# Gate/up RMS norm with squares summed by three token thirds and the factor spread from 96 partitions

## The reference

```
def rmsnorm(x, g):
    y = xf * lax.rsqrt(jnp.mean(xf * xf, axis=-1, keepdims=True) + EPS)
    return (y * g).astype(x.dtype)
def ffn_half(x, g, wg, wu, wd):
    h = rmsnorm(x, g)
    return x + 0.5 * ((jax.nn.silu(h @ wg) * (h @ wu)) @ wd)
```

## Time and profile before

| | us |
|---|---|
| runs | 2058.07, 2057.37, 2061.0 (median 2058.07) |
| profiled execution: its time | 2061.27 |
| its span, first to last instruction | 2059.5 |
| TensorE busy | 2031.5 (99%) |
| VectorE busy | 1683.0 (82%) |
| ScalarE busy | 978.1 (47%) |
| GpSimd busy | 359.7 (17%) |

### The profile page before, as it was taken

The page is one execution under the profiler, slowest core; times in us unless marked ns, Lnnn a source line. Parts: engine busy times, 40 slices in busy tenths (PEclk is TensorE's granted clock), DMA queues, the critical chain, the costliest instruction groups (busy, mean ns, idle before and its releaser), DMA issues. The chain is left out here.

```text
span 2059.5 us, 41110 instructions
## 1 busy us (share of the span) xinstructions
PE 2031.5 (99%) x15435; PEld 1975.0 (96%) x15435; DVE 1683.0 (82%) x2481; ACT 978.1 (47%) x1776; POOL 359.7 (17%) x219
## 2 busy tenths in 40 slices
PE   8999999999999999999989999999999999999998
PEld 7999999999889999999989999999997899999998
DVE  5999998756666999998899999976657589999975
ACT  6544453324545544463465655533345474444532
POOL 0322200033011222200022222001321112222000
PEclk8999999999999999999999999999999999999999
DMA  4232332352112222322223222324321122232331
GB/s 133 83 102 84 99 92 79 92 129 65 45 54 83 83 88 96 97 88 86 78 83 102 88 95 79 112 79 118 95 68 32 55 82 91 94 102 79 94 96 65
DMA packets 236727, 178.35 MB, mean 87 GB/s; under 512 B 35808, under 2 KB 231616, under 8 KB 236608
## 3 DMA queue, kind: packets, MB, share of 16 engines
q1 hardware_dynamic: 231712, 170.36, 27.8%
q10 hardware_dynamic: 4896, 6.36, 1.1%
HBM read 170.12 MB, written 3.62 MB: 84 GB/s over the span
## 5 line engine op out<-in xcount | busy, mean ns | idle before, releaser
L1471 PE MATMUL pair<-t_parts,chunk_high 128*128 128x288 f32 x4592 | 916.7, 295 | 6.3 <-POOL chunk_low L827 2.6
L1471 PEld LDWEIGHTS pair<-t_parts,chunk_high 128*128 128x128 f32 x4592 | 736.8, 188 | 8.0 <-POOL chunk_low L827 3.2
L1471 PE MATMUL pair<-t_parts,chunk_low 128*128 128x288 f32 x2296 | 677.7, 295 | 0.0
L1471 PEld LDWEIGHTS pair<-t_parts,chunk_low 128*128 128x128 f32 x2296 | 431.4, 188 | 0.0
L827 POOL TENSOR_TENSOR chunk_low<-set_raw,chunk_high 128x512 fp32r<-128x512 f32 x164 | 236.6, 1453 | 872.1 <-ACT chunk_high L926 872.1
L926 ACT ACTIVATE chunk_high<-chunk_sum 128x512 fp32r<-128x512 f32 x328 | 203.8, 630 | 372.5 <-DVE chunk_sum L2024 190.4
L821 POOL TENSOR_TENSOR w_low<-raw,w_high 128x1024 fp32r<-128x1024 f32 (+2 forms) x48 | 115.7, 2414 | 620.7 <-ACT w_high L874 620.7
L2036 DVE TENSOR_TENSOR chunk_low<-chunk_sum,chunk_high 128x512 fp32r<-128x512 f32 x328 | 214.5, 695 | 9.2 <-ACT chunk_high L926 1.9
L1418 PE MATMUL pair<-hidden_high,w_high 128*128 128x288 f32 x896 | 191.9, 296 | 0.0
L1418 PE MATMUL pair<-hidden_high,w_low 128*128 128x288 f32 x896 | 191.9, 296 | 0.0
L1418 PE MATMUL pair<-hidden_low,w_high 128*128 128x288 f32 x896 | 191.8, 296 | 0.0
(11 more groups left out here) (304 smaller groups left out, 3727.0 us busy)
## 6 DMA issues: line engine op xcount, KB each, us to landing
set_raw<-in_w_up_dram SPq DMA_DIRECT2D x44, 1024.0 KB, 5.3
set_raw<-in_w_gate_dram SPq DMA_DIRECT2D x44, 1024.0 KB, 5.3
raw<-in_w_down_dram SPq DMA_DIRECT2D x64, 448.0 KB, 3.8
down_raw<-in_w_down_dram SPq DMA_DIRECT2D x16, 1024.0 KB, 5.4
raw<-in_w_in_dram SPq DMA_DIRECT2D x20, 512.0 KB, 3.9
raw<-in_w_in_dram SPq DMA_DIRECT2D x16, 256.0 KB, 3.9
raw<-in_w_out_dram SPq DMA_DIRECT2D x8, 512.0 KB, 3.5
raw<-in_w_out_dram SPq DMA_DIRECT2D x16, 256.0 KB, 4.1
```

The lines of the kernel that those rows point to most:

```text
L1471: mm = nc.tensor.matmul(out, c[:, j, p, :], tr[p // 2][:, seat(p), x, t, :], start=p == 0 and n == 0, stop=p == KP - 1 and n == 2)
```

## The change

The tokens are cut into three thirds of 192 (`THIRD_T`). The sum of squares of third g goes to partitions 32g to 32g+31, 24 matmuls of 192 columns in place of 16 of 288. ScalarE takes the root of these 96 x 192 sums straight from PSUM into `sq_tmp`, in the place of the copy L1201. VectorE takes the reciprocal of 96 x 192 in place. Three matmuls spread it: the weights are one column of the identity (row 32g), read 128 times, the moving operand is `sq_tmp[0:96]`. The copy of partial sums, the matmuls L1537, the diagonals and the five matmuls with them go away. The positions of the reciprocal in VectorE's order and of the `keep_scale` copies in ScalarE's stay; the copies are cut at 384 tokens, not at 512, and need no factor. In the block phase `mean_square` is three matmuls on `sq_sum`, and the spread is two matmuls in the first part and one in the second.

```
-            def root(count, sums, parts):
+            def root(count, sums):
                 act.wait_ge(sum_done, 2 * count + 2)
-                nc.scalar.activation(root_tok[:, 0:4], sums[:, 0:4], ACT.Sqrt, bias=eps[:, 0:1], scale=float(parts)).then_inc(root_done, 1)
-                nc.scalar.activation(root_tok[0:DEC, 4:5], sums[0:DEC, 4:5], ACT.Sqrt, bias=eps[0:DEC, 0:1], scale=float(parts)).then_inc(root_done, 1)
-            def spread(count):
-                act.wait_ge(rms_ready, count + 1)
-                for t, (t0, n) in enumerate(TILES):
-                    ins = nc.scalar.activation(sq_tmp[0:n, t0:t0 + n], ident[0:n, 0:n], ACT.Copy, scale=root_tok[0:n, t:t + 1])
-                ins.then_inc(spread_made, 1)
+                nc.scalar.activation(sq_tmp[0:96, 0:THIRD_T], sums, ACT.Sqrt, bias=eps[0:96, 0:1]).then_inc(root_done, 2)
...
 (plain_tiles, ScalarE)
                 combined_of(0)
-                act.wait_ge(sum_done, 2 * ph + 1)
-                nc.scalar.activation(two(rms[0:96, :]), halves(3)[0:96], ACT.Copy).then_inc(parts_kept, 1)
+                root(ph, ps[3][0:96, 0, 0:THIRD_T])
                 free(3)
                 plain_chunks(q + 1, 1, 1)
...
                 combined_of(2)
-                root(ph, ps[ALONE][:, 0, 0:5], D_MODEL // 32)
                 combined_of(3)
-                spread(3 * layer + 2 * w)
                 chunk(q + 2, 0, A11)
...
+                def sum_thirds(pair, half, parts):
+                    for m, src in enumerate(parts):
+                        for g in range(3):
+                            mm = nc.tensor.matmul(ps[pair][32 * g:32 * g + 32, half, 0:THIRD_T], mean_d[:, 0:32], src[:, g * THIRD_T:(g + 1) * THIRD_T],
+                                                  start=m == 0, stop=m == len(parts) - 1)
+                    mm.then_inc(sum_done, 2)
+                def spread_thirds(part, pair, half):
+                    pe.wait_ge(rms_ready, 3 * layer + 2 * w + 1)
+                    for g in ((0, 1), (2,))[part]:
+                        col = (g % 2) * THIRD_T
+                        mm = nc.tensor.matmul(ps[pair][:, half, col:col + THIRD_T], ident[0:96, 32 * g:32 * g + 1].broadcast_to([96, P]),
+                                              sq_tmp[0:96, 0:THIRD_T], start=True, stop=True)
+                    mm.then_inc(scale_made, 1)
...
 (gate_up, TensorE)
+                    sum_thirds(3, 0, squares)
                     plain_tile(1, 0)
-                    pe.wait_ge(parts_kept, plain_before(layer, w) + 1)
-                    for t, (t0, n) in enumerate(TILES):
-                        mm = nc.tensor.matmul(ps[ALONE][0:n, 0, t:t + 1], rms[0:96, t0:t0 + n], mean_d[0:96, 0:1], start=True, stop=True)
+                    pe.wait_ge(root_done, 2 * ph + 2)
                     plain_tile(1, 1)
                     pe.wait_ge(left_made, set_number(layer, w, 0, 0) + 2)
-                    for t, (t0, n) in enumerate(TILES):
-                        dst = ps[FIRST][:, 0, t0:t0 + n] if t < 4 else ps[FIRST][:, 1, 0:n]
-                        mm = nc.tensor.matmul(dst, mean_d[0:n, :], sq_tmp[0:n, t0:t0 + n], start=True, stop=True)
+                    for part in range(2):
+                        spread_thirds(part, FIRST, part)
...
 (make_scale, VectorE)
-                nc.vector.reciprocal(root_tok[:, :], root_tok[:, :]).then_inc(rms_ready, 1)
+                nc.vector.reciprocal(sq_tmp[0:96, 0:THIRD_T], sq_tmp[0:96, 0:THIRD_T]).then_inc(rms_ready, 1)
```

More of the change, by code:

```diff
@@ L33 @@
 HALF = NT // 2
+THIRD_T = NT // 3
 KD = D_MODEL // P
@@ L926, in chunk @@
                 nc.scalar.activation(ch[:, j], src, ACT.Copy).then_inc(chunk_high, 1)
-            def root(count, sums, parts):
+            def root(count, sums):
                 act.wait_ge(sum_done, 2 * count + 2)
-                nc.scalar.activation(root_tok[:, 0:4], sums[:, 0:4], ACT.Sqrt, bias=eps[:, 0:1], scale=float(parts)).then_inc(root_done, 1)
-                nc.scalar.activation(root_tok[0:DEC, 4:5], sums[0:DEC, 4:5], ACT.Sqrt, bias=eps[0:DEC, 0:1], scale=float(parts)).then_inc(root_done, 1)
-            def spread(count):
-                act.wait_ge(rms_ready, count + 1)
-                for t, (t0, n) in enumerate(TILES):
-                    ins = nc.scalar.activation(sq_tmp[0:n, t0:t0 + n], ident[0:n, 0:n], ACT.Copy, scale=root_tok[0:n, t:t + 1])
-                ins.then_inc(spread_made, 1)
+                nc.scalar.activation(sq_tmp[0:96, 0:THIRD_T], sums, ACT.Sqrt, bias=eps[0:96, 0:1]).then_inc(root_done, 2)
             def keep_scale(ph, part, pair, half):
                 act.wait_ge(scale_made, 2 * ph + part + 1)
-                dst, src = (rms[:, 0:SEQ], ps[pair][:, 0, :]) if part == 0 else (rms[:, SEQ:NT], ps[pair][:, half, 0:DEC])
-                nc.scalar.activation(dst, src, ACT.Copy, scale=float(D_MODEL)).then_inc(rms_spread, 1)
+                dst, src = (rms[:, 0:2 * THIRD_T], ps[pair][:, 0, 0:2 * THIRD_T]) if part == 0 else (rms[:, 2 * THIRD_T:NT], ps[pair][:, half, 0:THIRD_T])
+                nc.scalar.activation(dst, src, ACT.Copy).then_inc(rms_spread, 1)
             def gate_up(layer, w, base_slot):
@@ L992, in during @@
                     if opens and b == 0:
-                        root(ph, ps[ALONE][:, 1, 0:5], 1)
+                        root(ph, ps[ALONE][0:96, 1, 0:THIRD_T])
                     for j in (S1, S2, S3, S4):
                         chunk(q + 1, 1 - b, j)
-                        if opens and b == 1 and j == S1:
-                            spread(3 * layer + 2 * w)
                         if opens and b == 1 and j == S4:
@@ L1477, in one_set @@
                             spread_scale(int(j == A22))
+                def sum_thirds(pair, half, parts):
[4 more added lines that the diff above has]
+                    mm.then_inc(sum_done, 2)
                 def mean_square():
                     pe.wait_ge(sq_added, 2 * KD * layer + 1)
-                    for t, (t0, n) in enumerate(TILES):
-                        mm = nc.tensor.matmul(ps[ALONE][0:n, 1, t:t + 1], sq_sum[:, t0:t0 + n], mean_d[:, 0:1], start=True, stop=True)
-                    mm.then_inc(sum_done, 2)
-                def spread_scale(part):
[L1488 to L1492, removed]
+                    sum_thirds(ALONE, 1, [sq_sum])
+                def spread_thirds(part, pair, half):
[5 more added lines that the diff above has]
+                    mm.then_inc(scale_made, 1)
+                def spread_scale(part):
+                    if part:
                         pe.wait_ge(rms_spread, 2 * ph + 1)
-                        mm = nc.tensor.matmul(ps[ALONE][:, 0, 0:DEC], mean_d[0:DEC, :], sq_tmp[0:DEC, SEQ:NT], start=True, stop=True)
-                    mm.then_inc(scale_made, 1)
+                    spread_thirds(part, ALONE, 0)
                 def plain_tile(b, n):
@@ L1525, in gate_up @@
                     pe.wait_ge(h_ready, x_count + KD)
[L1526 to L1532, removed]
-                    plain_tile(1, 0)
-                    pe.wait_ge(parts_kept, plain_before(layer, w) + 1)
-                    pe.wait_ge(left_made, set_number(layer, w, 0, 0) + 1)
-                    for t, (t0, n) in enumerate(TILES):
-                        mm = nc.tensor.matmul(ps[ALONE][0:n, 0, t:t + 1], rms[0:96, t0:t0 + n], mean_d[0:96, 0:1], start=True, stop=True)
-                    mm.then_inc(sum_done, 1)
+                    sum_thirds(3, 0, squares)
+                    plain_tile(1, 0)
+                    pe.wait_ge(root_done, 2 * ph + 2)
                     plain_tile(1, 1)
-                    pe.wait_ge(root_done, 2 * ph + 2)
-                    pe.wait_ge(spread_made, ph + 1)
                     pe.wait_ge(left_made, set_number(layer, w, 0, 0) + 2)
-                    for t, (t0, n) in enumerate(TILES):
-                        dst = ps[FIRST][:, 0, t0:t0 + n] if t < 4 else ps[FIRST][:, 1, 0:n]
-                        mm = nc.tensor.matmul(dst, mean_d[0:n, :], sq_tmp[0:n, t0:t0 + n], start=True, stop=True)
-                    mm.then_inc(scale_made, 2)
+                    for part in range(2):
+                        spread_thirds(part, FIRST, part)
                     one_set(1, 0)
```

3 lines of the change are left out of this document (1 added, 2 removed).

## The result

The changed kernel took 2063.64 us (median of 9 runs, 2061.78 to 2066.48), the kernel before 2057.62 us (9 runs, 2056.74 to 2061.0) on the same chip. The ratio is 1.003, 95% interval 1.0021 to 1.0039: slower by 0.3%, where 2056.6 us and no change had been forecast. The two profiled executions hide it: their spans are 2060.0 after and 2059.5 before, because before's took 2061.27 us, longer than any of its 9 runs, and after's 2061.78, its fastest.

A forecast was written before the change was run, and what follows sets the result against it. TensorE, busy 2031.5 of 2059.5 us, was taken as the bound, VectorE setting the block phase's pace. Three plain phases gaining 0.75 us each, less 0.8 in the block phase, gave -1.45, say 1.5: 2056.6 us, range 2052.8 to 2060.4.

The forecast's parts named there:

- The sums: TensorE, plain phase: 48 records run as 16 trios of 0.16, 2.6 us against 2.9 to 3.0, 0.4 us earlier.
- rival B: Sums on TensorE: three groups don't overlap at 192 columns, 3.9 us, 0.9 more than before; 2060.5 us; chance 0.08.
- The table load: ScalarE ahead of the root: the 1.28 us load runs before the wait, in idle time, so it hides.
- Root and reciprocal: Plain phase: ScalarE's root of 192 columns takes 0.42 us, VectorE's reciprocal of 192 columns 1.35 us.
- GpSimd's collision: Plain phase: GpSimd's second low part holds up VectorE's T3 low part, about 1.2 us lost; A12 gains 0.75, not 1.9.
- Rival A: GpSimd and VectorE in plain phases: their collision doesn't cost, A12 starts at 54.15; -5 us, 2053.1 us; chance 0.22.
- rival C: VectorE, plain and block phases: the reciprocal excludes GpSimd, A12 0.7 us late three times; +4.1 us, 2062.2 us; chance 0.08.
- The wait before A12: TensorE, each plain phase: waits about 1.9 us for ScalarE's copy, where 0.74 on GpSimd stood.
- a cover: TensorE's 1.9 us wait before A12, taken also as room for a slower weight load in the spread.
- The block phase: Longer reciprocal where VectorE has no room: A11 of the next set 0.8 us later; first copy's wait about 3 us.

The follow-up runs named there:

- the load in its place: Changed kernel with the root's semaphore increment 1 instead of 2, so the table load stands ahead of the wait: 2057.12 us, ratio 0.9995 to the kernel before.
- the held low part: On top of the root's increment of 1, GpSimd's low part of A12 held until VectorE's combination S2 is made, in plain phases: 2057.67 us, ratio 0.9999.
- Filled: Changed kernel plus small float32 matmuls on TensorE, 5 before A12 in each plain phase, 6 before the block phase's second spread: 2060.84 us, ratio 1.001.

## Why the prediction was wrong

The forecast was 1.5 us of gain; the loss was 6.0. Its steps:

- **The sums**: 2.6 us for the block forecast, 2.7 measured; the trios overlap. Right, rival B falls.
- **The table load**: the step that failed. "So it hides" was read off a root that carried its wait itself, and off idle time ahead of the copy. That there was time to hide it was right; that the load would use this time was not checked against the new instruction's form. The forecast did name the price, "if it ran behind the wait, 1.28 us would be lost": it measured 1.34, three times, 4.0 us. With the load in its place A12 came 0.95 us earlier by the trace, where 0.75 was forecast.
- **Root and reciprocal**: 0.42 and 1.34 us, forecast 0.42 and 1.35. With the load in its place the spread (1.14 us) waits for nothing, as forecast; with the load behind the sums it waited 0.85.
- **GpSimd's collision**: that the two engines hold each other up was right, who waits and for how long was not. It was to stretch the low part of T3 by 1.2 us; T3, T4 and S1 ran at their own pace, GpSimd's low parts took 1.97 us longer, and S2 was stretched by 0.92. Both stand ahead of the copies, so the effect on A12 was nearly the same. Rival A, that it costs nothing, falls by the held low part; rival C, that the reciprocal excludes GpSimd, falls with the reciprocal at 1.34.
- **The wait before A12**: forecast at 1.9 us, measured 1.99. That they agree is in part luck: the wait began and ended later than forecast, and with the load in its place it was 1.72. And it was priced as idle time alone and even called a cover. It was the clock's price that was missing: no term, bound or rival spoke of what TensorE's granted clock does behind such a wait. Filled, with all else equal, the kernel is 2.8 us faster by the medians.
- **The block phase**: 0.9 us by the trace against 0.8, and the wait "about 3 us" was 2.74. Here too the fall of the clock, about 1.4 us, came on top.

The sum, redone with what was measured: three plain phases at +0.39 us, the block phase at +0.9, and three falls at 1.4 to 1.5 us (the one near 1040 us costs nothing) give +6.3 to +6.6 us. The traces give +6.4 over the four phases, and 6.0 was measured between the medians. The profiled spans differ by only 0.5 us because the rest of the program hides 5.9: the early rise of the clock (1.46), and 2.8 and 1.6 us where the trace before has its own falls, near 472 us (with a wait of 2.40 us that was 1.56 after) and near 1551 us.

The Trainium skill, "TensorE: Matmul & The Clock Gate", section "HAM oscillation — how this bites in real kernels", tells of a kernel in which TensorE's waits between pieces of work bring the lower clock, so that each piece starts cold. The waits of that kernel are longer than those here, so it doesn't promise a fall behind 2 us. The traces show such falls, with 0.50 behind the waits that end at 55.01 and 1066.14 us, though not each time. Had it been weighed beside the forecast's own wait of 1.9 us, a slower rival could have stood there.

## What to carry to other kernels

Price a new wait of TensorE twice: its own length, and the granted clock behind it; look for places where the kernel before already waits two microseconds and read the clock after them, in more than one execution, since it falls in some and not in others. When an activation changes tables and waits, look in the trace at which of the two instructions, load or activation, has the wait; a small activation of the same table ahead of it puts the load where it is free. And before a chain is made shorter, look at which instruction ends the wait at its far end: here the order of two short copies was worth 6.6 us on top of the new form, which by itself, with the load in its place, was not clearly faster than the old one (1.0 us, inside the scatter); in the old form the same order brought nothing clear.

## What the runs showed of the hardware

- An activation with a wait and an increment of 2, where it needs a new table, had its wait on the table load; with an increment of 1 it stayed on the activation. 1.0 to 1.4 us a phase hung on it. Whether the chip or the making of the program puts the wait there was not looked into; an increment of 2 on other engines was not tried.
- The granted clock fell to 0.50 behind waits of about 2 us of an engine otherwise fully busy, not each time (5 of 9 at 1.98 to 1.99 us before A12), and matmuls of 288 columns went from 0.133 to 0.24 us. What decides between a fall and none was not found.
- A two-input combination of 0.69 us took 1.60 beside GpSimd's low parts and 0.69 without; the low part, 1.29 us at 59.27 in the earlier trace rows, took 1.77 beside VectorE.
- A float32 matmul of 224 columns left two records and took 0.37 us here ((55.67 - 53.84) / 5), against 0.133 for one of 288 columns of the rounded kind that the products use.
